# The second expert product: value rows as the moving operand, 512 columns at a time

## The reference

```
q = (xb @ w_pq).reshape(PEER_BLOCK, PEER_HEADS, 2, D_KEY // 2)
...
e = i1 * N_KEYS + i2
gate = jax.nn.softmax(best, axis=-1)
u = u_exp[e]
v = v_exp[e]
act = jax.nn.gelu(jnp.einsum("thkd,td->thk", u, xb))
return jnp.einsum("thk,thkd->td", (gate * act).astype(xb.dtype), v)
```

## Time and profile before

| | us |
|---|---|
| median of 3 runs | 2598.82 (2598.51 to 2599.08) |
| the profiled execution | 2607.07 |
| its span, first to last instruction | 2605.0 |
| PE busy, matmuls | 2330.1 (89%) |
| PE busy, weight loads | 2239.9 (86%) |
| VectorE busy | 1741.7 (67%) |
| ScalarE busy | 1291.1 (50%) |
| value stages, from the first to the last product | 916.1 to 1285.1 and 2229.0 to 2597.9 |

### The profile page before, as it was taken

The page is one execution under the profiler, slowest core; times in us unless marked ns, Lnnn a source line. Parts: engine busy times, 40 slices in busy tenths (PEclk is TensorE's granted clock), DMA queues, the critical chain, the costliest instruction groups (busy, mean ns, idle before and its releaser), DMA issues.

```text
span 2605.0 us, 53888 instructions
## 1 busy us (share of the span) xinstructions
PE 2330.1 (89%) x18096; PEld 2239.9 (86%) x18096; DVE 1741.7 (67%) x3632; ACT 1291.1 (50%) x2842; POOL 253.5 (10%) x286
## 2 busy tenths in 40 slices
PE   3887789999997699999889988799999976999998
PEld 3785579999996599999879946799999975999998
DVE  6665554888877955565633456638888869655555
ACT  3345244545556745455534554345555457545554
POOL 3000000000006900000010000000000049100000
PEclk7998789999998999999989979899999999999999
DMA  8761134555551055555434402345555520455554
GB/s 313 258 234 54 45 130 148 178 180 187 181 185 49 0 186 181 182 185 179 137 106 161 169 1 81 123 144 184 180 178 184 185 81 0 139 184 182 180 185 145
DMA packets 106072, 389.62 MB, mean 150 GB/s; under 512 B 12032, under 2 KB 12160, under 8 KB 105232
## 3 DMA queue, kind: packets, MB, share of 16 engines
q1 hardware_dynamic: 104688, 381.73, 42.8%
q10 hardware_dynamic: 992, 4.88, 0.5%
q0 software_dynamic: 320, 2.13, 0.2%
HBM read 387.64 MB, written 1.05 MB: 149 GB/s over the span
## 4 chain that ended last, share of the span: by engine, by line
PE 81%; POOL 8%; DVE 6%; ACT 3%; DMA 1%; issue 1%; SPq 0%; ACTq 0%; POOLq 0%; DVEq 0%
PE ps L533 19%; PE ps L502 16%; PE ps L497 16%; PE ps L499 15%; PE ps L537 9%; POOL scores L401 8%; DVE big L1113 1%; DMA big<-ada_in 1%; PE ps L612 1%; PE ps L592 1%; DVE act_lo L1166 1%; DVE lo L1090 1%; PE ps L602 1%; PE ps L640 1%; PE ps L491 1%
## 5 line engine op out<-in xcount | busy, mean ns | idle before, releaser
L827 ACT ACTIVATE hi<-raw 128x512 fp32r<-128x512 f32 x1356 | 776.2, 620 | 88.9 <-PE ps L502 87.1
L1090 DVE TENSOR_TENSOR lo<-raw,hi 128x512 fp32r<-128x512 f32 x844 | 551.7, 695 | 193.7 <-ACT hi L827 192.7
L497 PE MATMUL ps<-act_hi,hi 128*128 128x256 f32 x3376 | 557.6, 288 | 83.6 <-DVE act_lo L1166 41.8
L502 PE MATMUL ps<-act_hi,lo 128*128 128x256 f32 x3376 | 554.7, 287 | 26.1 <-DVE lo L1090 26.1
L497 PEld LDWEIGHTS ps<-act_hi,hi 128*128 128x128 f32 x3376 | 478.3, 197 | 90.2 <-DVE act_lo L1166 68.4
L499 PE MATMUL ps<-act_lo,hi 128*128 128x256 f32 x3376 | 553.4, 287 | 0.0
L533 PE MATMUL ps<-act_hi,hi 128*128 128x256 f32 x2048 | 513.9, 283 | 0.0
L533 PE MATMUL ps<-act_lo,hi 128*128 128x256 f32 x2048 | 513.5, 283 | 0.0
L502 PEld LDWEIGHTS ps<-act_hi,lo 128*128 128x128 f32 x3376 | 476.4, 196 | 28.9 <-DVE lo L1090 28.8
L499 PEld LDWEIGHTS ps<-act_lo,hi 128*128 128x128 f32 x3376 | 476.9, 196 | 0.0
L852 ACT ACTIVATE big<-ps 128x256 f32 (+1 forms) x354 | 135.8, 383 | 592.1 <-PE ps L502 592.1
(11 more groups left out here) (176 smaller groups left out, 1361.5 us busy)
## 6 DMA issues: line engine op xcount, KB each, us to landing
raw<-u SPq DMA_DIRECT2D x256, 512.0 KB, 3.3
raw<-v SPq DMA_DIRECT2D x256, 512.0 KB, 3.4
raw<-front SPq DMA_DIRECT2D x166, 512.0 KB, 3.2
big<-ada_in SPq DMA_DIRECT2D x48, 512.0 KB, 5.5
big<-biasA_in ACTq DMA_DIRECT2D x1, 2048.0 KB, 10.2
xT<-xT_in ACTq DMA_DIRECT2D x1, 1024.0 KB, 9.4
big<-keys_in ACTq DMA_DIRECT2D x1, 1024.0 KB, 13.6
scores<-memT_in POOLq DMA_DIRECT2D x1, 1024.0 KB, 6.7
```

Source lines behind the costliest of these rows:

```text
L497: pe.matmul(out_ap, hi_l(k), hi_r(k), start=(first and k == 0), stop=False, skip_group_check=True)
L502: mm = pe.matmul(out_ap, lo_l(k), hi_r(k), start=False, stop=(last and k == n - 1), skip_group_check=True)
L827: act.activation(hi[:, s, :, :], raw[:, rs, 4 * h:4 * h + 4, :], ACT.Copy).then_inc(hi_done, 1)
L1090: dve.tensor_tensor(lo[:, s, :, :], raw[:, rs, 4 * h:4 * h + 4, :], hi[:, s, :, :].bitcast(F32), ALU.subtract).then_inc(lo_done, 1)
```

## The change

The operands of the second expert product swap places. The stationary operand is now 128 experts x 128 tokens of act_hi or act_lo, the moving operand a whole half of value rows, 512 columns. Per half there are two token tiles with two products of hi and one of lo: 6 matmuls of 512 columns instead of 12 of 256. The sums in PSUM are then [128 tokens, 1024 columns] per token tile, in the same four banks: `vsum[tt][half]` is bank 2 + 2·half + tt. The reader of the sums needs them transposed, so at the end of a stage VectorE copies token tile 0 and ScalarE token tile 1 to `vout` (two instructions of 128x512 each), PE turns the 16 blocks of 128x128 back into `acc`, bank by bank, and VectorE adds as before, waiting for each bank.

```
+        vsum = [[ps[:, 2 + 2 * half + tt, :] for half in range(2)] for tt in range(QT)]
+        vout = cut(4096, QT, D)
...
-                    for k in range(4):
-                        for w, a in ((hi, act_hi), (hi, act_lo)):
-                            pe.matmul(acc[:, k0 + k, :], w[:, s, k, :], a[:, b, :], start=False, stop=False,
+                    w_hi = hi[:, s, :, :].rearrange("p k c -> p (k c)")
+                    w_lo = lo[:, s, :, :].rearrange("p k c -> p (k c)")
+                    for tt in range(QT):
+                        for a in (act_hi, act_lo):
+                            pe.matmul(vsum[tt][h], a[:, b, tt * P:tt * P + P], w_hi, start=False, stop=False,
                                       skip_group_check=True)
                     wait_lo()
-                    for k in range(4):
-                        mm = pe.matmul(acc[:, k0 + k, :], lo[:, s, k, :], act_hi[:, b, :], start=False, stop=False,
+                    for tt in range(QT):
+                        mm = pe.matmul(vsum[tt][h], act_hi[:, b, tt * P:tt * P + P], w_lo, start=False, stop=False,
                                        skip_group_check=True)
...
                 run(f"v{b}")
+                for half in range(2):
+                    pe.wait_ge(v_taken[0], 2 * (b - 1) + half + 1)
+                    pe.wait_ge(v_taken[1], 2 * (b - 1) + half + 1)
+                    for d in range(4 * half, 4 * half + 4):
+                        for tt in range(QT):
+                            mm = pe.transpose(acc[:, d, tt * P:tt * P + P], vout[:, tt, d * P:d * P + P], ident[:, :])
+                        if d % 2:
+                            mm.then_inc(v_turned, 1)
...
                 groups(act, r, body)
+                act.wait_ge(used, r.half0 + 2 * r.units)
+                for half in range(2):
+                    act.activation(vout[:, 1, 512 * half:512 * half + 512], vsum[1][half], ACT.Copy)\
+                        .then_inc(v_taken[1], 1)
...
                 dve.wait_ge(used, r.half0 + 2 * r.units)
+                for half in range(2):
+                    dve.tensor_copy(vout[:, 0, 512 * half:512 * half + 512], vsum[0][half]).then_inc(v_taken[0], 1)
...
             for d in range(KT):
+                dve.wait_ge(v_turned, d // 2 + 1)
                 ins = dve.scalar_tensor_tensor(out=xT[:, d, :], in0=acc[:, d, :], scalar=mod[:, 40 + d:41 + d],
...
             for d in range(KT):
+                dve.wait_ge(v_turned, KT // 2 + d // 2 + 1)
                 ins = dve.tensor_tensor(xT[:, d, :], acc[:, d, :], xT[:, d, :], ALU.add)
```

More of the change, by code:

```diff
@@ L301, in two_blocks_kernel @@
         ahi, alo = sem("dense_hi"), sem("dense_lo")
+        v_taken = [sem("v_sums_taken_dve"), sem("v_sums_taken_act")]
+        v_turned = sem("v_sums_turned")
         out_s = sem("out_stored")
```

## The result

The changed kernel takes 2570.22 us (median of 4 runs, 2567.24 to 2572.46), the kernel before 2598.95 beside it; the ratio is 0.9886 (95% interval 0.9869 to 0.9903). It is faster by 28.7 us, not by 67.4, and lies above the range of 2523 to 2565. In the pair of profiled executions the difference is 2607.07 − 2572.46 = 34.6 us. The parts of the program outside the value stages vary by several us between executions of one kernel: v1's first product started at 915.3 us in one profile of the changed kernel and at 911.7 in another.

The account below looks back on a forecast made before the run. The prediction took the tensor engine's own pace in the two value stages as the bound; −74.0 (product) + 1.4 + 5.2 (tails) = −67.4 us, from the median 2598.82 to 2531.4 us, range 2523 to 2565 for 8 in 10.

Parts of the forecast that it names:

- The tails: End of both value stages: new copies and turns before the additions cost 5.2 us in the first, 1.4 in the second.
- the queues that were named: Stage ends: ScalarE's squares wait behind its copies (5.2 us); VectorE's additions wait for copies and PE's turns (1.4 us).
- The feed: Value stages: ScalarE, VectorE and transfers keep up with 2.59 us a unit, costing nothing; rival of 25.6 us lost, chance 0.06.
- ScalarE's wait for PE: Value stages: the wait before act_hi was to shrink from 1.42 to about 1.1 us.
- The pace of the product: Value product on PE: 512-column matmuls hide their loads, a stage takes 331.9 us instead of 368.95, −74.0 us in both.
- I take 216.1 ns: Value product: start-to-start time chosen for a 512-column fp32r matmul, between bounds of 213.3 and 240.2 ns.
- fixed cost: Rival, value product: 13.4 ns belong to each matmul, so 226.7 ns each, −34.8 us with tails, 2564 us; chance 0.08.
- The estimate that the prediction worked out from it: Value product by the skill's formula: a unit from 2.621 to 2.590 us, 8 us in all, about the tails' cost.

Follow-up runs that it names:

- e2: Changed kernel with each 512-column product split into two of 256 on the same stationary tile: 2608.93 us, ratio 1.0021 to the kernel before.
- e3: Changed kernel with ScalarE's table load and squares ahead of its copies at the first stage's end, second table load dropped: 2564.47 us, ratio 0.9846.
- e1: Kernel replaced by bursts of 96 matmuls, one form each, computing none of the reference: fp32r 226.7 ns at 512 columns, 119.9 at 256.
- e5: The changed kernel timed again, unaltered, in a later session: 2568.09 us, ratio 0.9865 to the kernel before.
- e11: Kernel before, with its own roles and tails, value product operands split into packed bf16 hi and lo parts: 2537.47 us, ratio 0.9751.
- e8: Changed kernel with all value product operands split into packed bf16 hi and lo parts, 16 bits kept: 2535.61 us, ratio 0.9740.
- e4: Matmul bursts in place of the kernel, with steps in the moving operand: bf16 512 columns 216.0 ns packed, 225.9 with columns 4 bytes apart.
- e6: Changed kernel with the value rows' lo part as packed bf16, times a bf16 view of act_hi: 2577.82 us, ratio 0.9901.

## Why the prediction was wrong

- *The tails*: right. +5.15 and +1.44 measured against +5.2 and +1.4, by the queues that were named; e2 gives 4 to 5.5 us for both by time. What it did not see is that PE's own queue lay just below ScalarE's, so that e3 won back only half.
- *The feed*: right. No wait of PE in the stages, ScalarE's wait for PE 1.26 us before act_hi (forecast 1.1 for a shorter unit).
- *The pace of the product*: wrong, and it is the step that failed. "I take 216.1 ns" should have been 226.7: 1536 × 10.6 ns = 16.3 us a stage, 33 us in both, all of the error in the profiled pair. The step from 120.1 to 216.1 for twice the columns took the loads for exposed; they were hidden before too (e1: 111 ns for a load and a short stream, 119.9 for the stream of 256). The price was among the rivals (fixed cost, 2564 us, given 0.08), and the profiled pair gave its −34.8 us to 0.2. By the medians the gain was 28.7 us, and 36.7 in the session of e5; the kernel before lay at 2598.5 to 2602.5 us in the first and mostly at 2604 to 2606 in the second, so the rest is spread between sessions.
- *Why it was mis-sized*: two readings supported each other, and both were false. The first took the order "load 0.11, matmul, 0.01, load" of the earlier trace rows for a bound by the load. A load that starts right behind each matmul looks the same when the stream is the bound; e1 has a full load and its matmul within 111 ns, and the stream of 256 columns at 120. The second took fp32 rows for the price of an fp32r stream of equal length. They had the same cycles, but read 4 bytes in two cycles and not in one. The half clock row, an fp32r stream without the cost, differs in the same way.
- The rival's mechanism, a fixed cost per matmul, is right for fp32r of 256, 320, 384 and 512 columns at full clock (448 took 11 ns more than it says). Its cause, as far as shown: it appears when columns lie 4 bytes apart at one column per cycle (fp32r, stepped bf16), and not with 2 bytes, with 4 bytes at two cycles a column (fp32), or at half clock. Which part of the read path does it is not shown.
- The Trainium skill's formula for the warm gap (TensorE: Matmul & The Clock Gate, "Back-to-back issue gap", N/2.4 + 2.5) held to 0.1 ns for bf16 at 256 columns in e1 (109.2). The estimate that the prediction worked out from it, 8 us gained and as much lost in the tails, came true in bf16 (e11's stages are 4.0 us longer than e8's, twice), not in fp32r.

## What to carry to other kernels

Before a price is borrowed from another row, compare bytes per cycle, not only cycles: an estimate for a form that the trace does not show needs a row with the same type. When a load follows each matmul without a gap, ask how short load and matmul can get together (a narrow stream shows it) before calling the load the bound. In fp32r fewer, wider matmuls pay 13.4 ns each less; with packed bf16 operands the 4 us a stage that were left went into the tails.

## What the runs showed of the hardware

- fp32r at full clock: columns/2.4 GHz + 13.2 to 13.5 ns for 256, 320, 384 and 512 columns, the stationary tile new or the same (e1, e4); 448 columns took 211.0 ns, and a load of 32 columns made it 231.9 at 512. bf16 and fp32 records: + 2.5 to 2.7 ns.
- fp32r and bf16 moving columns 8 bytes apart take twice the time of columns 4 bytes apart (453 against 226.7 ns and 452 against 225.9 for 512, e4).
- fp32r with 128 columns and a full load each goes at 111.1 ns a matmul; bf16 with 128 columns at (291.93 − 286.60)/96 = 55.5 ns with a full load each (e1).
- Mixing bf16 matmuls into an fp32r sequence left the stage 1.6 us longer where 5.5 less was due, some 14 ns a change if the change is the cause (e6).
